# Attention of a two-block transformer: score tiles rotate over three pairs of PSUM banks, and TensorE's turn is reordered

## The reference

```
q_n, kc, vc, ks, vs, kw, vw, gates, q_s, k_s, v_s, q_f, k_f, v_f, f = split(rms_norm(x) @ w_in[i])
o_nsa = gate0 * compressed_attn + gate1 * softmax(q k_sel) v_sel + gate2 * softmax(q k_win) v_win  # 8 heads, 2 kv heads
o_sb  = stick_breaking(q_s, k_s, v_s)      # 4 heads: exp(log_beta + reversed cumsum of log(1 - beta)), strictly causal
o_fox = softmax(q_f k_f + c_q - c_k) v_f   # 4 heads, c = cumsum(log_sigmoid(f))
x = x + concat(o_nsa, o_sb, o_fox) @ w_out[i]
x = x + softmax(q_m k_mem) v_mem @ w_mo[i] # 4 heads over a memory of 256 rows
x = x + conv_gated_mlp(rms_norm(x)) @ ...
```

## Time and profile before

| | |
|---|---|
| median of 3 runs | 1657.5 us (1654.69 to 1657.87) |
| profiled execution | 1662.66 us, its span 1661.0 us, mean TensorE clock 0.987 of full speed |
| TensorE matmul (PE) busy | 1598.3 us, 96% |
| VectorE (DVE) busy | 1181.4 us, 71% |
| ScalarE (ACT) busy | 796.4 us, 48% |
| GpSimd (POOL) busy | 120.0 us, 7% |
| DRAM traffic | 293.59 MB, 177 GB/s mean |

### The profile page before, as it was taken

One profiled execution on the slowest core, in us unless ns is written; L12 is line 12 of the kernel. 1 busy time (PEld: TensorE's weight loads), 2 busy tenths in 40 slices (PEclk: granted clock), 3 DMA queues, 4 the chain that ended last, 5 costly groups with the idle time before them and its releaser, 6 DMA issues.

```text
span 1661.0 us, 36188 instructions
## 1 busy us (share of the span) xinstructions
PE 1598.3 (96%) x12317; PEld 1480.0 (89%) x12324; DVE 1181.4 (71%) x1780; ACT 796.4 (48%) x1271; POOL 120.0 (7%) x125
## 2 busy tenths in 40 slices
PE   8999899999999989999999999999999999999998
PEld 6987679999897768999979878889999989999997
DVE  4774778888897468998867454468767678677654
ACT  4556456653355546665455222224555345455533
POOL 3100111110310011110000000000000000000000
PEclk8999999999999999999999999999999999999999
DMA  8440434558665034556935543348555765545551
GB/s 325 165 153 3 163 102 166 175 174 273 251 226 196 16 114 165 177 177 234 364 110 172 173 163 127 115 164 304 189 178 188 244 204 184 177 161 180 181 185 51
DMA packets 81014, 293.59 MB, mean 177 GB/s; under 512 B 9008, under 2 KB 10544, under 8 KB 80176
## 3 DMA queue, kind: packets, MB, share of 16 engines
q1 hardware_dynamic: 78768, 283.31, 49.7%
q10 hardware_dynamic: 2176, 9.31, 1.6%
HBM read 291.53 MB, written 1.05 MB: 176 GB/s over the span
## 4 chain that ended last, share of the span: by engine, by line
PE 72%; DVE 13%; ACT 8%; issue 5%; DVEq 1%; ACTq 1%; DMA 0%; SPq 0%; POOL 0%
PE projs L1586 37%; PE accs L1586 29%; PE ob L1586 5%; ACT WH L466 4%; DVE WL L914 3%; DVE us L1242 2%; DVE cv L1251 1%; DVE cv L1249 1%; ACT AH L529 1%; PE projs L1813 1%; DVE rstd L1011 1%; ACT FH L502 1%; DVE ring L924 1%; DVE scr L1087 0%; DVE nmax L1066 0%
## 5 line engine op out<-in xcount | busy, mean ns | idle before, releaser
L914 DVE TENSOR_TENSOR WL<-ring,WH 128x1024 fp32r<-128x1024 f32 x436 | 541.7, 1245 | 271.3 <-ACT WH L466 269.9
L466 ACT ACTIVATE WH<-ring 128x1024 fp32r (+1 forms) x436 | 460.0, 1056 | 572.4 <-PE projs L1586 298.4
L1586 PE MATMUL projs<-AH,WH 128*128 128x256 f32 (+2 forms) x2304 | 579.7, 294 | 25.5 <-ACT AH L529 8.3
L1586 PE MATMUL projs<-AL,WH 128*128 128x256 f32 (+2 forms) x2304 | 562.3, 288 | 0.3
L1586 PEld LDWEIGHTS projs<-AH,WH 128*128 128x128 f32 x2304 | 430.8, 191 | 47.3 <-ACT AH L529 13.8
L1586 PEld LDWEIGHTS projs<-AL,WH 128*128 128x128 f32 x2304 | 429.6, 192 | 10.2 <-DVE AL L1028 4.5
L1586 PE MATMUL projs<-AH,WL 128*128 128x256 f32 (+2 forms) x2304 | 328.2, 285 | 0.0
L1586 PEld LDWEIGHTS projs<-AH,WL 128*128 128x128 f32 x2304 | 299.0, 189 | 3.2
L1586 PE MATMUL accs<-FH,WH 128*128 (+1 forms) x768 | 190.5, 284 | 2.0 <-ACT WH L466 2.0
L1586 PE MATMUL accs<-FL,WH 128*128 (+1 forms) x768 | 189.7, 281 | 0.0
L1586 PEld LDWEIGHTS accs<-FH,WH 128*128 128x128 f32 x768 | 144.3, 188 | 3.3 <-issue 3.3
(11 more groups left out here) (249 smaller groups left out, 1754.0 us busy)
## 6 DMA issues: line engine op xcount, KB each, us to landing
ring<-in_stream SPq DMA_DIRECT2D x532, 512.0 KB, 3.3
W1v<-in_w ACTq DMA_DIRECT2D x2, 1024.0 KB, 5.1
W1k<-in_w ACTq DMA_DIRECT2D x2, 1024.0 KB, 8.8
D<-in_decay ACTq DMA_DIRECT2D x4, 512.0 KB, 5.7
x<-in_xT SPq DMA_DIRECT2D x2, 512.0 KB, 5.3
memT<-in_memT SPq DMA_DIRECT2D x1, 1024.0 KB, 11.6
ctxT<-in_ctxT ACTq DMA_DIRECT2D x1, 1024.0 KB, 8.3
out_y<-ybuf SPq DMA_DIRECT2D x8, 128.0 KB, 2.0
```

Source lines behind the costliest of these rows:

```text
L466: A(WH[:, s, :], ring[:, r % RING, :], ACT.Copy).then_inc(wh_ready, 1)
L914: V.tensor_tensor(WL[:, s, :], ring[:, r % RING, :], WH[:, s, :].bitcast(F32), ALU.subtract).then_inc(consumed, 1)
L1586: return T.matmul(out, lhsT, rhs, start=start, stop=stop, skip_group_check=True)
```

## The change

Three things change, all in `attend` and its helper.

- `scores_of(u)` rotates over three pairs of banks: the two pairs of `accs` and, for `u % 3 == 2`, `projs`.
- A softmax unit's transposes go to the unit's own score banks, no longer to `projs`; ScalarE's `turned_copy` reads there. `turn(v)` no longer waits for `pt_ready` of the unit before. `scores(v)` no longer waits for `exp_ready` of unit `v - 2`, but for `pt_ready` of unit `v - 3`.
- TensorE issues three score tiles ahead of the loop (two where there are two units), and in the loop `turn(v)`, `values(v - 1)`, `scores(v + 2)`. The filler matmuls go to `ob[0]`.

The programs of VectorE, ScalarE and GpSimd keep their order.

```diff
--- before.py
+++ after.py
@@ -388,7 +388,7 @@
             return ((0, 0, 256), (1, 256, 256)) if un["kind"] == "full" else ((0, 0, 128), (1, 128, 256))
 
         def scores_of(u):
-            return accs[:, 2 * (u % 2):2 * (u % 2) + 2, :]
+            return projs if u % 3 == 2 else accs[:, 2 * (u % 3):2 * (u % 3) + 2, :]
 
         def prob_of(u):
             return scr[:, 4 * (u % 2):4 * (u % 2) + 4, :].rearrange("p (g a) n -> p g (a n)", g=2)
@@ -619,7 +619,7 @@
                     if un["kind"] == "stick":
                         A(PT[:, u % 2, :, 0:w], scores_of(u)[:, :, 0:w], ACT.Exp).then_inc(pt_ready, 1)
                     else:
-                        A(PT[:, u % 2, :, 0:w], projs[:, :, 0:w], ACT.Copy).then_inc(pt_ready, 1)
+                        A(PT[:, u % 2, :, 0:w], scores_of(u)[:, :, 0:w], ACT.Copy).then_inc(pt_ready, 1)
 
                 def out_block(v):
                     act.wait_ge(pv_done, u0 + v + 1)
@@ -1760,8 +1760,8 @@
                 def scores(v):
                     u, un = u0 + v, units[v]
                     score = scores_of(u)
-                    if v >= 2:
-                        pe.wait_ge(exp_ready, softs[v - 2])
+                    if v >= 3:
+                        pe.wait_ge(pt_ready, u - 2)
                     Q, K_ = (mq, mk) if un["kind"] == "full" else (P, P)
                     if un["kind"] == "stick":
                         for j0, c in ((0, 0), (128, 256)):
@@ -1805,12 +1805,10 @@
                         ins.then_inc(t_mm, 1)
                         return
                     pe.wait_ge(p_ready, softs[v])
-                    if u >= 1:
-                        pe.wait_ge(pt_ready, u)
                     blocks = ((0, 0), (128, 256), (256, 128), (384, 384)) if un["kind"] == "full" else ((0, 0), (128, 128), (256, 256))
                     for g in range(2):
                         for src, dst in blocks:
-                            ins = T.transpose(projs[:, g, dst:dst + 128], prob[:, g, src:src + 128], ident)
+                            ins = T.transpose(scores_of(u)[:, g, dst:dst + 128], prob[:, g, src:src + 128], ident)
                     ins.then_inc(t_mm, 1)
 
                 def values(v):
@@ -1832,15 +1830,15 @@
                     if un["ends"]:
                         n["o"] += 1
 
-                scores(0)
-                scores(1)
-                turn_over(fill, proj[0])
+                for v in range(min(U, 3)):
+                    scores(v)
+                turn_over(fill, ob[0])
                 for v in range(U):
-                    if v + 2 < U:
-                        scores(v + 2)
                     turn(v)
                     if v:
                         values(v - 1)
+                        if v + 2 < U:
+                            scores(v + 2)
                 values(U - 1)
                 n["u"] += U
                 n["soft"] = softs[-1]
```

## The result

The changed kernel takes 1725.86 us (median of 4 runs, 1725.23 to 1727.06) where the kernel before took 1657.68 us beside it. The ratio is 1.0404, with a 95% interval from 1.0381 to 1.0427: 68 us slower. 1733 us was forecast, with a range of 1701 to 1766.

The account below looks back on a forecast made before the run. It took TensorE, 72% of the chain of waits, to bound the kernel, with VectorE almost as full beside it. Ring +43, memory attention -2.3 and clock +34.5 gave +75 us on the median 1657.5: 1733 us, range 1701 to 1766.

Parts of the forecast that it names:

- The ring: Attentions of 12 units: TensorE and VectorE wait for each other in turn, 5.44 or 6.29 us a step.
- eight steps: Layer 0, transposes of unit 1 to those of unit 9: 50.3 us in place of 28.55, +21.8 us.
- The forecast's cost of both attentions at full clock: Both attentions of 12 units, without any fall of the clock: +43 us.
- The signs named beforehand: Before transposes: some 16 idle stretches of 2.6 to 2.9 us, released by VectorE's product, some 45 us.
- Nothing overtakes on VectorE: VectorE's program: a waiting instruction holds back ready work behind it, as with fox units, where VectorE idled 2.79 us.
- no ring: faster: Rival: VectorE has the next product before turning to the maxima, so only removed waits count: 5.8 us less, 1652 us; chance 0.02.
- The removed waits: Attention of 12 units: at most 1.7 us given back. Memory attention: 1.21 us a layer, both layers -2.3 us.
- The clock: TensorE's clock falls to half level behind idle stretches in the attentions of 12 units, swinging: +34.5 us.
- the rows at 2.18 and 2.39 us: Idle TensorE stretches before the change: two of three, 2.18 us in layer 1 and 2.39 before memory transposes, dropped the clock.
- half of 69 us: Clock price in both attentions: 69 us if TensorE's part of each step ran at half clock throughout; half taken, 34.5.
- two far ends: Clock price in both attentions: nothing at full clock throughout, 69 us with TensorE's part at half clock throughout.
- The full-clock rival: Attentions of 12 units: the ring holds but the clock stays up, 1698 us, up to 1706 with short spells; chance 0.09.

Follow-up runs that it names:

- The kernel with the clock held: The changed kernel plus 20 matmuls on zeros behind the scores of each step, in TensorE's idle stretch: 1703.36 us, ratio 1.0276.
- the values last: The changed kernel with TensorE's turn as transposes v, scores v+2, values v-1: 1688.18 us, ratio 1.0166.
- the banks alone: The changed kernel with its three pairs of banks and own-bank transposes, but TensorE's old order: 1656.12 us, ratio 0.9976.

## Why the prediction was right

**The ring** is what happened, at its place and at its size. The kernel with the clock held shows it bare. The forecast had eight steps of 5.96, 5.44, 6.29, 5.44, 6.29, 8.15, 8.80 and 3.95 us; measured between transposes are 5.96, 5.53, 6.29, 5.53, 6.28, 8.24, 8.81 and 4.07. The forecast's cost of both attentions at full clock was +43 us; 70.97 and 72.28 us against 48.51 and 49.48 are +45.3, of which 1.6 us is still clock, at the first stick unit of layer 1. The signs named beforehand came too: fourteen waits of 2.66 to 3.00 us before transposes, seven in a layer, released by VectorE's product; with the shorter ones such waits come to 45.5 us.

**Nothing overtakes on VectorE**: the maxima waited 3.4 us and more in the changed kernel, with the next unit's work behind them, and moving them in VectorE's program took 53 us off by the medians. The rival "no ring: faster" named the right point, since it is the order of `second` and `first` that decides, but it needed an overtaking that the engine does not do. Even with the order moved, the kernel is slower than before: VectorE then has the maxima only one unit ahead, and waits 1.79 us for ScalarE's exponentials in a step. The old order on both sides keeps two units ahead.

**The removed waits** gave nothing in the attention of 12 units. Turning back the order and keeping the banks leaves it at 98.8 us against 98.0, and puts a new wait of 0.90 us in each layer, which the changed kernel does not have. In the memory attention they gave 1.9 us a layer, where 1.2 was forecast. That term was too small by the clock, which comes back before the values, eight of which take 1.08 us: the mean clock of the memory attention is 0.87 where it was 0.77. Why it comes back sooner was not tried apart from the wait, and stays open.

**The clock** is the term that was mis-sized. It fell, as the rows at 2.18 and 2.39 us had suggested, in both layers, behind idle stretches of 2.66 to 3.0 us. The price was put at half of 69 us, 34.5. The changed kernel and the filled one are 14.2 us apart in layer 0 and 10.3 in layer 1: 24.5 us, a third of the 69, and 22.5 or 25 us by the medians. With the 1.6 us that the filled kernel still lost, some 26. The step that failed is taking the middle between two far ends with only three idle stretches to go by: that the clock comes back under scores of fox units and slowed pieces was seen, but how often could not be read from the trace before. Between 0.80 and 0.81 of mean clock, about two fifths of the time in the attentions was at the half level.

The Trainium skill (TensorE: Matmul & The Clock Gate, section "Why this matters for your kernels") asks for no idle stretch over about 3 us. By that rule the clock would have stayed up; in layer 0 it fell behind the first stretch of 2.66 us. The full-clock rival's 1698 us is what the filled kernel comes near (1703) only with work put into the gaps.

**The sum**: 45.3 for the ring, 24.5 for the clock and -3.8 for the memory attentions are 66 us in the profiled executions; the medians differ by 68. Forecast were 43, 34.5 and -2.3, together 75. So the time came out 7 us below the forecast: the clock was put 10 us too high, the ring 2 us too low, and the gain of the memory attentions 1.5 us too small.

## What to carry to other kernels

When an engine's order is changed, write down beside it the order of every engine that it feeds: an in-order engine that waits for a new item holds back finished work behind it, and two engines that overlapped then take turns. More buffers do not help if the program issues the item later; here the third pair of banks allowed no more lookahead than the two had (with the old order a score tile waited 0.90 us for the copy in front of it), and the new order took one unit away. An idle stretch of TensorE can have a second price in the clock, and fillers in it take that back without touching its cause.

## What the runs showed of the hardware that was not expected

- The clock fell behind idle stretches of 1.7 to 1.9 us where one of 0.75 to 1.9 us came in every step (mean clock 0.90 and 0.92 with the values last). With stretches of 1.1 to 1.5 us in the steps and one of 2.03 us behind the fox units (VectorE's order moved) it fell in layer 0 only behind the latter, and layer 1 kept the full clock:

```profile
528.77:584.86 56.09, 45.38 (x374) 31.79 (x374) 30.05 (x78) 33.18 (x106) 1.27 (x2) 1.00 0.12 46
```

- The length of one idle stretch does not decide alone, and what does was not found. The matmuls of the first stick unit took 3.62 us in layer 1 before and 2.02 in layer 0; with the banks alone they took 2.62 us in layer 0 and 2.02 in layer 1, behind idle stretches of 2.0 to 2.2 us in all four. Behind the 2.39 us before the memory transposes eight of them took 1.77 us in layer 0 before and 1.09 in layer 1 with the banks alone. A difference of a microsecond and a half between two attentions of one profiled execution each need not be an effect of the edit.
- Filler matmuls on zeros held the clock (1.00 in layer 0, where it was 0.80) at no cost to the path that the trace shows, since they ended before the awaited product: twenty of 256 columns took 2.35 us in a gap of 2.8.
- The clock came back under transposes alone: with the memory units' own banks its mean was 0.61 in the first microsecond of the sixteen transposes (from 204.4), 0.50 in the two behind it and 1.00 under the values (from 208.1), and TensorE had nothing but the transposes between.
